# A macaron encoder layer on one Trainium2 core: the first weights of the modulation in quarters, products block by block, and tile 6 moved between blocks of the mixer entry

## What is computed

```python
mods = (silu(c) @ w_ada + b_ada).reshape(1, 9, 1024)      # w_ada 1024 x 9216
def sublayer(h, j, fn, w):
    shift, scale, gate = mods[:, 3*j], mods[:, 3*j+1], mods[:, 3*j+2]
    u = layer_norm(h) * (1 + scale) + shift
    z = 2**0.25 * h + w * gate * fn(u)
    return layer_norm(z) * ln_g[j] + ln_b[j]
h = sublayer(x, 0, swiglu1, 0.5)      # (silu(u @ gate) * (u @ up)) @ down, width 2816
h = sublayer(h, 1, mixer, 1.0)        # u @ w_in, dilated and 2-D neighbourhood attention, @ w_out
h = sublayer(h, 2, swiglu2, 0.5)
```

## Time and profile before

| | us |
|---|---|
| median of 3 runs (lowest, highest) | 1976.26 (1975.4, 1978.62) |
| the profiled execution | 1979.03 |
| its span on the core | 1977.2 |
| TensorE busy in the span | 1902.4 (96%) |
| VectorE, ScalarE, POOL busy | 1228.4, 834.0, 605.5 |

### The profile page before, as it was taken

One profiled execution on the slowest core, in us unless ns is written; L12 is line 12 of the kernel. 1 busy time (PEld: TensorE's weight loads), 2 busy tenths in 40 slices (PEclk: granted clock), 3 DMA queues, 4 the chain that ended last, 5 costly groups with the idle time before them and its releaser, 6 DMA issues. The chain is left out here.

```text
span 1977.2 us, 26739 instructions
## 1 busy us (share of the span) xinstructions
PE 1902.4 (96%) x9698; PEld 1528.0 (77%) x9698; DVE 1228.4 (62%) x1987; ACT 834.0 (42%) x1459; POOL 605.5 (31%) x432
## 2 busy tenths in 40 slices
PE   6999999999999989999999998989999999999997
PEld 4778888887888766777678876778888888888886
DVE  5876766665697863444535556688444444457888
ACT  4533333333445663443435554265333333334543
POOL 0253443343960010000043230003534434449500
PEclk9999999999999999999999998999999999999999
DMA  9256565556874421110043113532333332368733
GB/s 332 68 197 195 178 211 162 182 184 215 303 260 119 139 94 44 54 33 32 12 115 69 43 43 107 192 107 62 120 107 95 118 107 86 118 223 295 247 107 117
DMA packets 164667, 271.42 MB, mean 137 GB/s; under 512 B 13012, under 2 KB 83768, under 8 KB 164408
## 3 DMA queue, kind: packets, MB, share of 16 engines
q1 hardware_dynamic: 153888, 235.18, 36.0%
q10 hardware_dynamic: 9624, 30.39, 4.9%
q0 software_dynamic: 1024, 4.13, 1.2%
HBM read 211.73 MB, written 57.93 MB: 136 GB/s over the span
## 5 line engine op out<-in xcount | busy, mean ns | idle before, releaser
L1720 PE MATMUL f_ps<-f_uh,f_ops 128*128 128x512 f32 x2496 | 775.5, 391 | 8.3 <-DVE f_ul L1531 1.9
L1720 PEld LDWEIGHTS f_ps<-f_uh,f_ops 128*128 128x128 f32 x2496 | 469.4, 188 | 112.0 <-issue 10.1
L1720 PE MATMUL f_ps<-f_ul,f_ops 128*128 128x512 f32 x1248 | 486.4, 390 | 0.0
L1082 POOL TENSOR_TENSOR f_sums<-f_raw 128x512 f32<-128x512 f32 x80 | 112.1, 1402 | 529.8 <-DMA f_raw<-in_ffn_w_gate 232.3
L1720 PEld LDWEIGHTS f_ps<-f_ul,f_ops 128*128 128x128 f32 x1248 | 234.6, 188 | 48.3
L1579 DVE TENSOR_TENSOR f_dl<-f_blocks,f_dh 128x1024 fp32r<-128x1024 f32 (+1 forms) x146 | 207.5, 1438 | 69.4 <-ACT f_dh L1289 69.3
L1289 ACT CAST f_dh<-f_blocks 128x1024 fp32r<-128x1024 f32 (+1 forms) x146 | 144.3, 990 | 215.9 <-PE f_ps L1850 213.0
L1403 DVE TENSOR_TENSOR f_ops<-f_sums,f_ops 128x512 fp32r<-128x512 f32 x160 | 125.5, 784 | 119.8 <-ACT f_ops L1143 119.5
L1850 PE MATMUL f_ps<-f_dh 128*128 128x512 f32 x496 | 193.1, 389 | 0.8 <-DVE f_ev L1616 0.8
L1850 PE MATMUL f_ps<-f_dl,f_dh 128*128 128x512 f32 x496 | 193.0, 389 | 0.0
L1850 PE MATMUL f_ps<-f_dh,f_dl 128*128 128x512 f32 x496 | 193.0, 389 | 0.0
(11 more groups left out here) (284 smaller groups left out, 3073.5 us busy)
## 6 DMA issues: line engine op xcount, KB each, us to landing
f_hidden<-acc SPq DMA_DIRECT2D x154, 256.0 KB, 4.3
f_blocks<-f_hidden SPq DMA_DIRECT2D x154, 256.0 KB, 3.3
f_blocks<-in_ffn_w_down SPq DMA_DIRECT2D x132, 256.0 KB, 5.4
f_raw<-in_ffn_w_gate SPq DMA_DIRECT2D x20, 1024.0 KB, 6.2
f_raw<-in_ffn_w_up SPq DMA_DIRECT2D x20, 1024.0 KB, 5.5
f_aw<-in_w_ada ACTq DMA_DIRECT2D x28, 512.0 KB, 4.1
acc<-in_w_ada ACTq DMA_DIRECT2D x28, 512.0 KB, 3.9
in_raw<-in_w_in SPq DMA_DIRECT2D x24, 512.0 KB, 4.0
```

The costliest lines, as they stand in the source:

```text
L1082: nc.gpsimd.tensor_tensor(sums[:, x], of, with_, how).then_inc(s_done, 1)
L1720: done = nc.tensor.matmul(ps[:, bank, :], l[:, k, :], r[:, k, :], start=fresh and k == 0 and m == 0, stop=closed and k == HK - 1 and m == ...
```

## The change

**1. Quarters.** `w_ada` comes in four quarters of 256 features of shift and scale, each in four loads of 512 KB that cover four feature blocks in rows of 1 KB (before: two blocks in rows of 2 KB). The bytes, the 64 matmuls of 1x256 and their PSUM banks stay (quarter 0 in bank 0, the others in bank 5); `take`, `turn_rows` and `add_bias` run four times, each for 4 columns of `mod_col`; there is one more PSUM memset.

**2. The order of the loads.** SP: x 0 to 3, quarter 0, weights part 0, quarters 1 and 2, weights part 1, x 4 to 7, quarter 3. The 16 stores of the table are issued by POOL and wait for the last load of quarter 3; POOL's sums of weights come behind them and wait also for all tiles normalised and all four quarters.

**3. Products block by block.** `plain_slice(kk, k)` does block k for the four products of group kk (12 matmuls), so that a block is multiplied when its quarter is there. Sums, row turns and turns stand between the slices. The banks of the turns differ. All eight turns of the second half stand together ahead of product 8 and wait for the last quarter.

**4. Tiles 4 to 7 in the beginning.** Statistics and coefficients of tiles 4 to 7, and their normalising on ScalarE, come ahead of the modulation of blocks 6 and 7.

**5. Mixer entry.** Tile 7's `deviation` stands between the high parts of blocks 4 and 5 on ScalarE; VectorE does the coefficients and the affine step of tile 6 at block 5; tile 6 is entered by ScalarE behind the cast of weight part 1, the root and the coefficients then cover tiles 4, 5 and 6 together (their root at the end of the first network goes), and these three are normalised ahead of tile 7's statistics. The low part of weight part 0 is made by VectorE instead of POOL.

The diff, cut to its core:

```diff
-    def load_w(self, sp, h, i):
-        if h == 1:
-            sp.wait_ge(self.summed, i + 1)
-        view = self.w_ada[:, 2 * i:2 * i + 2, 0:M_FIRST].rearrange("p k (s n) -> p k s n", s=2)
-        for s in range(2):
-            sp.dma_start(self.mem.first_w[i][:, :, s, :], view[:, :, s, NB * h:NB * h + NB]
-                         ).then_inc(self.w_ld[4 * h + i], 16)
+    def load_w(self, sp, q):
+        for c in range(2):
+            if q >= 2:
+                sp.wait_ge(self.summed, 2 * (q - 2) + c + 1)
+            view = self.w_ada[:, HK * c:HK * c + HK, 0:M_FIRST].rearrange("p k (s n) -> p k s n", s=2)
+            for s in range(2):
+                sp.dma_start(self.mem.first_w[2 * (q % 2) + c][:, :, s, :], view[:, :, s, 2 * P * q:2 * P * q + 2 * P]
+                             ).then_inc(self.w_ld[2 * q + c], 16)
...
-    def store_table(self, sp):
-        sp.wait_ge(self.neg, 1)
+    def store_table(self, pool):
+        pool.wait_ge(self.neg, 1)
+        pool.wait_ge(self.w_ld[2 * QUARTERS - 1], 32)
...
+            def plain_slice(kk, k, these=range(4)):
+                pe.wait_ge(lo0, HK * kk + k + 1)
+                u = (B11, B21)[kk]
+                for n in these:
+                    o = 4 * kk + n
+                    pe.wait_ge(w_lo, o + 1)
+                    _, _, j, f = plain(o)
+                    wh, wl = op(o)
+                    for m, (l, r) in enumerate(((wh, uh), (wh, ul), (wl, uh))):
+                        done = nc.tensor.matmul(ps[:, PLAIN_BANK[0][j][f], :], l[:, k, :], r[:, u, k, :],
...
+                plain_slice(0, 3)
+                plain_slice(1, 0)
+                begin.add_products(pe, ps, 3, 0)
+                begin.add_products(pe, ps, 3, 1)
+                plain_slice(1, 1, (0, 1))
+                begin.turn_rows(pe, ps, 3)
+                turn(6)
+                turn(7)
+                plain_slice(1, 1, (2, 3))
+                plain_slice(1, 2)
+                plain_slice(1, 3)
+                for y in range(KT, 2 * KT):
                     turn(y)
+                for p in range(RING, PLAIN):
+                    plain_product(p)
...
-        @block.gpsimd
-        def _(pool):
-            pool.wait_ge(w_hi, 3)
-            nc.gpsimd.tensor_tensor(wl[:, :, 0, :], raw[:, :, 0, :], wh[:, :, 0, :].bitcast(F32),
-                                    ALU.subtract).then_inc(q_lo, 1)
...
+                    if y == 5:
+                        closing.coefficients(dve, 6)
+                        closing.affine(dve, 6)
```

More of the change, by code:

```diff
@@ L326, in set_bias, with bank_of, add_products @@
                                      ALU.add).then_inc(self.bias_set, 1)
[L328 to L337, removed]
+    def bank_of(self, q):
+        return 0 if q == 0 else 5
+    def add_products(self, pe, ps, q, c):
+        bank = self.bank_of(q)
+        if c == 0:
+            if q < 2:
+                pe.wait_ge(self.zeroed, 1 if q == 0 else 3)
+                pe.wait_ge(self.c_ready, 1)
+            else:
+                pe.wait_ge(self.columns, q)
+        pe.wait_ge(self.w_ld[2 * q + c], 32)
+        for k in range(HK * c, HK * c + HK):
+            for j in range(2):
@@ L457, in _ @@
                 ent.square(act, t, acc[:, t, :])
-            ent.root(act, 6, 8)
-            for t in (6, 7):
-                ent.normalise(act, t, acc[:, t, :], 3)
+                ent.root(act, first, t + 1)
+            split(2)
+            for y in range(5):
+                high(y)
+            closing.deviation(act, 7, ent.nrm[7])
+            for y in range(5, KT):
+                high(y)
+            split(1)
+            entering(6, 4)
+            split(0)
+            for t in (4, 5, 6):
+                ent.normalise(act, t, acc[:, t, :], 2)
+            entering(7, 7)
+            ent.normalise(act, 7, acc[:, 7, :], 3)
             for y in range(KT, 2 * KT):
@@ L527, in _ @@
             split(1, 2)
-            ent.coefficients(dve, 4, 6, 2)
-            for t in (6, 7):
-                closing.coefficients(dve, t)
-                closing.affine(dve, t)
-            ent.coefficients(dve, 6, 8, 3)
+            ent.coefficients(dve, 4, 7, 2)
+            split(0, 3)
+            closing.coefficients(dve, 7)
+            closing.affine(dve, 7)
+            ent.coefficients(dve, 7, 8, 3)
             blocks(1)
@@ L839, in op_at, with turn_bank, turned_before @@
             return at[j, i] - SPARE
+        def turn_bank(y):
+            if begin is not None and y < KT:
+                return TURN[0][y % 3]
+            return TURN[y // KT][y % 4]
+        def turned_before(y):
+            return max((x for x in range(y) if turn_bank(x) == turn_bank(y)), default=None)
         def half1(y):
```

200 lines of the change are left out of this document (110 added, 90 removed).

## The result

The changed kernel takes 1981.2 us in the median of 21 runs (1978.57 to 1985.37), the kernel before 1976.18 in 21 runs beside it (1972.28 to 1980.31): ratio 1.0025, 95% interval 1.0019 to 1.0031, that is 5.0 us slower (3.8 to 6.1). The forecast was 1978.1, 1.8 us slower, in a range from 1971.5 to 1984.0: the sign and that range hold, the forecast's own narrower range, 1975 to 1980.2, does not.

A forecast was written before the change was run, and what follows sets the result against it. TensorE, busy 96% of the span, was taken as the bound, so only its waits can be given back. Beginning +4.8 and mixer entry -3.0 made +1.8 us on 1976.26: 1978.1, range 1971.5 to 1984.0, the forecast's own 1975 to 1980.2.

The forecast's parts named there:

- The loads: Beginning: 16 loads of `w_ada` in 1 KB rows cost 2.6 us more; last landing at 46.3 (43.7 to 51.9).
- T: Beginning: the time when all 16 stores of the table are in, forecast at 63.1 us.
- The table: Beginning, the deciding term: 16 stores, 0.73 MB at 54 GB/s, take 13.6 us behind the last quarter and hold ScalarE.
- The 0.7 in this term: Beginning: 1 MB loads on SP meet the table's stores on half of the queues, costing 0.7 us, up to 5.4.
- the first rival: Beginning: table stores on POOL's queue spread over 16 engines, 8.4 us, T = 57.2; total -1.9, 1974.4; chance 18%.
- The rival that has VectorE hold the issues: Beginning: table stores take 19.2 us instead of 13.6, T = 68.7; total +7.2; chance 18%, shared with a late last quarter.
- TensorE's path: Beginning: TensorE's own work is no limit; without the table's limit product 8 starts at about 64.3, 1.1 later than before.
- ScalarE's chain: Beginning: modulations and casts from T on, then three matmuls, end product 8 at T + 7.7 = 70.8.
- The beginning in sum: Beginning: product 8 ends at 70.8 instead of 66.0, +4.8 us.
- The mixer entry: Mixer entry: second half's turns start 2.0 us earlier, the clock that stays gives 1.0; -3.0 taken, bounds -0.5 to -4.3.
- the mixer gain fails: Mixer entry: a new idle ahead of 704.8 lets the clock fall; -0.5 instead of -3.0, total +4.3, 1980.6; chance 10%.
- The bound of 65.2 for T: Beginning: if T is later than 65.2, the sum passes +3.95 us, the 0.2% a measurement can tell.

The follow-up runs named there:

- four_rows: The changed kernel with a quarter's sums as four 1x128 matmuls into four groups of PSUM rows instead of two 1x256 into two: 1979.5 us.
- order: The changed kernel with blocks 6 and 7 modulated and split ahead of normalising tiles 6 and 7, last sums taken ahead of tile 7's statistics: 1979.4 us.
- highs: The changed kernel with ScalarE's four high parts that product 8 needs put ahead of the table's wait and the four others: 1978.2 us.

## Why the prediction was right or wrong

**The loads: right.** Last landing forecast at 46.3, measured 47.0 (a slip in the working, 0.73 MB for a table of 0.75, changes T by 0.3 only); 1.5 us for 512 KB in rows of 1 KB is 350 GB/s, measured 348.

**The table: right in size, wrong in rank.** T was forecast at 63.1, 16.8 us behind the last landing. Where it could be seen, in four_rows, the DMA released ScalarE at 64.10, 16.9 behind it. The 0.7 in this term for the weight loads beside the stores is shown by no run by itself. The queue didn't matter, 53 GB/s at a DMA share of 0.49, before 54 at 0.46: the first rival (a faster queue) fell, though its 8.4 us for the issues came true (8.42; 16 steps of 504 ns would be 8.1). The rival that has VectorE hold the issues fell too: none took over 0.71 us. But ScalarE was not waiting for the table. That the total still came out inside the range is luck: another path happened to end only 0.7 us behind the one that the forecast had worked out.

**TensorE's path: the step that failed.** I wrote that from the last landing on TensorE "has 1 us of sums, 42 matmuls of slices (9.8) and two and eight turns (some 4.9), up to 62", and so it would "start product 8 at about 64.3". It started at 67.84. Three things were missing. The sums: I took 16 matmuls at 1.0, but a whole quarter of 32 was left to do and at half the rate, 3.62; four_rows takes 3.9 us off the turns' start. The order on ScalarE and VectorE: the last row taken behind tile 7's statistics, and the blocks 6 and 7 behind the normalising of the tiles 6 and 7, 1.9 us in the experiment `order`. And the eight turns in one piece: the 7.7 us of ScalarE's chain, which I counted behind T alone, come behind the turns as well (64.83 to 72.8), with no product left to cover them, where before product 7 lay between two groups of turns. So this path ended 0.7 us later than the table would have, and both ended far behind 66.

**The beginning in sum:** forecast +4.8, measured +6.7 at the end of product 8: ScalarE's chain began at 64.83 and not at 63.1, and took 8.0 us and not 7.7. At the wait for ScalarE it is +7.0 between the two profiles and +7.6 between the means, (108.3 + 109.9) / 2 = 109.1 for the changed beginning and 101.5 for the five traces with the old one.

**The mixer entry: the mechanism right, the size half.** The wait at 718 and L233's 2.17 went, as forecast, and the second half's first turn came 26.4 us behind the phase's first (26.7 forecast). But the old order takes less than the one profile showed: by the means 1.0 us was won there and not 2.0, and 0.5 behind it for the clock that stays and not 1.0. The forecast had `deviation(7)` delay the cast of part 1 by 1.9; the delay came earlier and through VectorE, 2.73 us for block 4 behind tile 6's affine step, a step I had not put on the path.

**The sum:** 4.8 - 3.0 = +1.8 forecast; by the traces' means 7.6 - 1.5 = +6.1, and the medians show 5.0 (3.8 to 6.1), the difference lying in the rest past 737 or in the small number of traces. The rival "the mixer gain fails" was half true, and by both of its parts: a new wait, and the clock that falls to 0.61 behind it. The bound of 65.2 for T was not passed, ScalarE started at 64.83; the sum passed +3.95 because the mixer entry gave half.

What stays open: what decides whether the clock falls at product 8 and behind the new wait in the mixer entry; and why the first quarter's 32 matmuls take 5.0 to 6.5 us, which sets the start of the slices at 22.0 to 23.8, while the profile shows a clock of 1.00 and the later quarters take 3.62.

## What to carry to other kernels

Before a large matmul phase is cut into finer pieces, look at how the small matmuls share TensorE: a piece that leaves fewer groups of output rows in use costs more per row, and that shows in a timeline only if rows of the same count are compared. When the forecast rests on one late wait, work out the next limit with the same care; here two limits lay 0.7 us apart, and removing either alone (four_rows, highs) moved the end of product 8 by 0.6 to 0.7 us, both together by 4.7. A loss counts only at the next wait that all versions share: 1.3 us lost at product 8 were gone 35 us later. And where a wait of TensorE or a clock differs between two profiles, look at the same stretch in other executions of the same code before it is put down to the change.

## What the runs showed that was not expected

- 32 matmuls of the sums (one output row, 256 columns) take 1.91 us with four groups of PSUM rows in use and 3.62 with two; the order among the four groups makes no difference (1.93).
- An idle of TensorE of 1.90 us ahead of product 8 is followed by a granted clock of 1.00 in one execution and of 0.57 (some 3 us at 1.2 GHz) in another, of the same instructions there.
- A wait of 2.0 to 2.7 us of TensorE in the mixer entry is followed by a granted clock of 0.60 to 0.67 over 4 us in nine traces and of 1.00 in one.
- While POOL subtracts or adds large tiles, a step of VectorE on 128x2 or 128x3 takes 2.17 to 2.39 us instead of 0.17, and two low parts of 128x512 take 2.39 together instead of 1.3.
